# Expert panels of 1,792 features, a new block order and ring fill, and an fp32 first tile in the last gate

## The reference, cut to what matters

```python
def moe_swiglu(x, w_router, w_gate, w_up, w_down):
    logits = (x @ w_router).astype(jnp.float32)
    top_vals, top_idx = lax.top_k(logits, TOP_K)              # 2 of 8 experts
    weights = jax.nn.softmax(top_vals, axis=-1)
    ...
    for e in range(N_EXPERTS):
        out = out + combine[..., e:e + 1] * swiglu(x, w_gate[e], w_up[e], w_down[e])

# behind it, for layer i:
h = layer_norm(ALPHA * h + f, ln_g[i, 1], ln_b[i, 1])
h = h + jax.nn.sigmoid(h @ ple_w_gate[i] + ple_b_gate[i]) * (p[i] @ ple_w_proj[i])
```

## Time and profile before

| | us |
|---|---|
| three runs | 1474.23, 1474.25, 1471.96; median 1474.23 |
| the profiled execution | 1470.26 |
| its span, first to last instruction | 1468.5 |
| TensorE busy in the span | 1412.5 (96%) |
| VectorE busy | 702.5 (48%) |
| ScalarE busy | 319.8 (22%) |
| bytes moved by DMA | 467.99 MB, mean 319 GB/s |

### The profile page before, as it was taken

The page is one execution under the profiler, slowest core; times in us unless marked ns, Lnnn a source line. Parts: engine busy times, 40 slices in busy tenths (PEclk is TensorE's granted clock), DMA queues, the critical chain, the costliest instruction groups (busy, mean ns, idle before and its releaser), DMA issues.

```text
span 1468.5 us, 27721 instructions
## 1 busy us (share of the span) xinstructions
PE 1412.5 (96%) x12131; PEld 925.5 (63%) x12131; DVE 702.5 (48%) x1128; ACT 319.8 (22%) x432; POOL 24.6 (2%) x51
## 2 busy tenths in 40 slices
PE   8999999999999999999999999999999999999687
PEld 7888788888778877356666664456454454465135
DVE  4795678878874668432332332241422322323247
ACT  4444344344455553000000000000000000000012
POOL 3010000000000000000000000000000000000100
PEclk9999999999999999999999999999999999999998
DMA  9956445555456126999999999999999999999980
GB/s 367 337 197 248 165 172 183 189 200 185 166 177 207 50 78 262 419 412 404 416 414 419 420 419 420 419 418 421 419 419 420 419 420 419 420 420 415 417 348 30
DMA packets 135481, 467.99 MB, mean 319 GB/s; under 512 B 8524, under 2 KB 9376, under 8 KB 134848
## 3 DMA queue, kind: packets, MB, share of 16 engines
q1 hardware_dynamic: 130864, 450.92, 77.9%
q0 software_dynamic: 2992, 12.70, 2.3%
q10 hardware_dynamic: 1504, 2.62, 0.5%
HBM read 462.53 MB, written 3.67 MB: 317 GB/s over the span
## 4 chain that ended last, share of the span: by engine, by line
PE 78%; DMA 13%; DVE 5%; ACT 2%; issue 1%; SPq 1%; POOL 0%; ACTq 0%; POOLq 0%; DVEq 0%
PE ps L1781 76%; DMA ring<-in_moe_w_up_dram 10%; DMA ring<-in_moe_w_down_dram 2%; DMA raw<-in_ple_w_gate_dram 1%; DVE split L1121 1%; PE ps L1799 1%; ACT split L751 1%; DVE h L1169 1%; DVE stats L1173 1%; DVE acc L1164 1%; DVE htl L1136 0%; SPq L578 0%; PE ps L2116 0%; PE ps L2152 0%; DVE acc L1216 0%
## 5 line engine op out<-in xcount | busy, mean ns | idle before, releaser
L1781 PE MATMUL ps<-ring,xt 128*32 128x448 f32 x5632 | 546.2, 542 | 25.9 <-DMA ring<-in_moe_w_up_dram 25.6
L1781 PEld LDWEIGHTS ps<-ring,xt 128*32 128x32 f32 x5632 | 256.7, 110 | 300.0 <-issue 242.1
L1781 PE MATMUL ps<-split,hth 128*128 128x512 f32 x1168 | 366.7, 395 | 6.0 <-DVE htl L1136 2.8
L1699 DVE TENSOR_TENSOR m_hb<-ps,m_sg 128x224 f32<-128x224 f32 x88 | 29.2, 385 | 575.8 <-ACT m_sg L1054 575.8
L1781 PE MATMUL ps<-ring,m_bt 128*32 128x256 f32 (+1 forms) x3472 | 278.4, 469 | 6.8 <-DMA ring<-in_moe_w_down_dram 6.7
L1781 PEld LDWEIGHTS ps<-split,hth 128*128 128x128 f32 x1168 | 218.9, 190 | 53.8 <-DVE htl L1136 3.4
L1781 PEld LDWEIGHTS ps<-ring,m_bt 128*32 128x32 f32 x3472 | 173.0, 110 | 108.7 <-issue 28.8
L1781 PE MATMUL ps<-split,htl 128*128 128x512 f32 x584 | 229.3, 393 | 0.0
L1707 DVE STREAM_TRANSPOSE m_bt<-m_hb 32x224 f32<-32x224 f32 x352 | 205.1, 583 | 5.5
L1054 ACT ACTIVATE m_sg<-ps 128x224 f32<-128x224 f32 x88 | 25.4, 357 | 727.7 <-PE ps L1781 727.7
L1121 DVE TENSOR_TENSOR split<-raw,split 128x2048 fp32r<-128x2048 f32 x52 | 118.7, 2291 | 64.0 <-ACT split L751 63.9
(11 more groups left out here) (256 smaller groups left out, 651.1 us busy)
## 6 DMA issues: line engine op xcount, KB each, us to landing
ring<-in_moe_w_gate_dram SPq DMA_DIRECT2D x128, 896.0 KB, 17.2
ring<-in_moe_w_up_dram SPq DMA_DIRECT2D x128, 896.0 KB, 16.6
ring<-in_moe_w_down_dram SPq DMA_DIRECT2D x128, 896.0 KB, 16.2
raw<-in_gm_w_in_dram SPq DMA_DIRECT2D x14, 1024.0 KB, 14.6
raw<-in_ffn_w_gate_dram SPq DMA_DIRECT2D x14, 1024.0 KB, 5.0
raw<-in_ffn_w_up_dram SPq DMA_DIRECT2D x14, 1024.0 KB, 5.0
raw<-in_ffn_w_down_dram SPq DMA_DIRECT2D x14, 1024.0 KB, 5.0
raw<-in_fox_w_in_dram SPq DMA_DIRECT2D x12, 1024.0 KB, 4.9
```

The lines of the kernel that those rows point to most:

```text
L1699: ins = nc.vector.tensor_tensor(m_hb[:, q, :], ps[bank][:, QTR:2 * QTR], m_sg[:, q, :], ALU.mult)
L1781: return nc.tensor.matmul(o, a, b, start=start, stop=stop)
```

## The change

- **Panels.** `PANEL` goes from 896 to 1,792. There are 16 blocks instead of 32. A ring slot is one row of 1,792 floats for each of 128 partitions: before, a gate or up load filled a slot with two rows of 896 (256 input features); now it fills it with one row of 1,792 (128 input features). The bytes of a load and the loads of the down rows stay as they were. All gate slots of a block now stand ahead of its up slots, so gate and up have PSUM banks of their own (`gate_banks`, `up_banks`; a wide block's third up group reuses bank 0 after the silu of it). `m_hb` is gone: DVE writes the product back into `m_sg`. `m_bt` is single (only the last block has one of its own), so `turn_hidden(b)` waits for `down(b-1)`, and the silu of block `b` waits for `turn_hidden(b-1)`.
- **Order and gathering.** The first block of expert 6 is second, its other block seventh. The half of `xt` that holds experts 0, 6, 1 and 2 is gathered ahead of block 0; the other half behind `gate_up(1)`. `acc = ALPHA * h` is made behind that.
- **Fill.** `xh` lies over `acc` and `xl` over `par_b`; ring slots 13 to 15 wait for the router's logits (`lg_full`) instead of the gather; the first 16 loads are issued in the order `FILL`. `xh` and `xl` are made ahead of or within the routing.
- **The last gate.** Token tile 0 is copied unrounded (`ht`) and multiplied by `raw` in plain fp32; tile 1 stays a split product with four pairs `split1`. The tiles' norms stand directly behind each other on DVE, and a Sqrt ahead of `y_last` loads ACT's table early.

```diff
-PANEL = 896
+PANEL = 1792
-    SLOT = 2 * PANEL
-    X_BLK = 12
+    SLOT = PANEL
+    X_BLK = 24
...
+        order = [(e, j) for e in range(BIG) for j in range(NPAN)]
+        order.insert(1, (BIG, 0))
+        order.insert(6, (BIG, 1))
+        return order + [(NE - 1, j) for j in range(NPAN)]
...
-    xh, nxt = at("xh", [P, T, D], F32R, hth_at)
-    xl, _ = at("xl", [P, T, D], F32R, nxt)
+    xl, _ = at("xl", [P, T, D], F32R, par_b_at)
+    xh, _ = at("xh", [P, T, D], F32R, ph)
...
+    FILL = (0, 1, 2, 3, 4, 5, 10, 11, 12, 6, 7, 8, 9, 13, 14, 15)
...
             if end > SPLIT_END[-1]:
-                sp.wait_ge(gx_full, 2 * KD)
+                sp.wait_ge(lg_full, T)
...
+        act.wait_ge(s0["h"], H_NORM3 + 2)
+        nc.scalar.copy(xh[:, 0, :], h[:, 0, :]).then_inc(xh_ready, 1)
         tile_hi(1)
+        act.wait_ge(s0["h"], H_NORM3 + 2 * T)
+        nc.scalar.copy(xh[:, 1, :], h[:, 1, :]).then_inc(xh_ready, 1)
         small_out(3, 4, NE, slice(P, S))
...
             def turn_hidden(b):
+
                 dve.wait_ge(e_hid, hid0 + (b + 1))
+                if 0 < b < NB - 1:
+                    dve.wait_ge(s0["used"], used0 + (G_MOE + down_at(b - 1) + 8))
...
+                for which, banks in enumerate((gate_banks(b), up_banks(b))):
+                    for k in range(KD):
+                        slot = landed(gu_at(b) + which * KD + k)
                         for q, bank in enumerate(banks):
+                            if which == 1 and k == 0 and bank in gate_banks(b):
+                                pe.wait_ge(e_silu, silu0 + (3 * b + gate_banks(b).index(bank) + 1))
...
+                    gate_up(b)
+                    if b == HALF_1:
+                        pe.wait_ge(route_ready, 1)
+                        gather(1, at_e, gx0)
                         pe.wait_ge(gx_act, gx0 + KD)
                         pe.wait_ge(gx_dve, gx0 + KD)
...
+        def last_ple():
+
+            st = streams[1]
+            for nb in range(2):
+                bank = ps[GATE_BANKS[nb]]
+                for k in range(KD):
...
+                    last = mm(bank[:, :], ht[:, k, 0:P], raw[:, 2 * nb + k // 4, k % 4, :], k == 0, k == KD - 1)
+                last.then_inc(last_gate, 1)
+                if nb == 0:
+                    last_turn(1)
```

More of the change, by code:

```diff
@@ L891, in projected, with ple @@
                     .then_inc(proj_copied, 1)
-        def ple(which, g0, ready, last):
-            st = streams[which]
+        def ple(g0, ready, last):
+            st = streams[0]
             for nb in range(2):
@@ L1055, in experts @@
                         .then_inc(e_silu, 4 - len(banks) if q == len(banks) - 1 else 1)
+                if b == HALF_1:
+                    gathered(1, gx0)
+                if b == HALF_1 and r is None:
+                    act.wait_ge(gx_full, 2 * KD)
+                    for m in range(T):
+                        nc.scalar.mul(acc[:, m, :], h[:, m, :], ALPHA).then_inc(acc_init, 1)
                 if b and ORDER[b - 1][1] == NPAN - 1:
@@ L1204, in norm @@
                     scale_bias(h, acc, m, part, par[:, 2 * n + 1, part]).then_inc(streams[which]["h"], 1)
-            for q in range(2):
-                stream_lo(q, T - 1, which)
+            if which == 0:
+                for q in range(2):
+                    stream_lo(q, T - 1, which)
         def residual(k, g_end):
@@ L1413, in ple @@
                     if n < last:
[L1414 to L1426 removed]
+                        rest_lo(n)
@@ new lines, in ple @@
+                part = slice(nb * W, (nb + 1) * W)
+                dve.wait_ge(st["used"], g0 + 2 + 2 * nb)
+                for m in range(T):
+                    nc.vector.tensor_tensor(sig[:, m, part], ps[2 * (1 - nb) + m][:, :], ple_b[:, 0, part], ALU.add)\
+                        .then_inc(st["gb"], 1)
+                for m in range(T):
+                    dve.wait_ge(st["gs"], nb * T + m + 1)
+                    seq(nc.vector.tensor_tensor(sig[:, m, part], sig[:, m, part], pp[:, m, part], ALU.mult))
@@ L1608, in _ @@
         by_place(slots[:, :, 0:NE], slots_e)
-        def first_experts(half):
-            return slice(4 * half, 4 * half + 4)
-        select_every(first_experts, (0,))
-        rest_x(0)
-        select_every(first_experts, (1,))
+        for half in range(2):
+            select_half(half, lambda e, n: slice(e, e + n))
         def route_weights():
@@ L1741, in _ @@
             with dve.Fori(1, ROUNDS) as r:
-                rest_x(dve.snap(r * T))
-                select_every(lambda half: bass.ds(dve.snap(r * NE + 4 * half), 4))
-                gathered(r)
+                for m in range(T):
+                    rest_x(dve.snap(r * T), m)
+                for half in range(2):
+                    select_half(half, lambda e, n: bass.ds(dve.snap(r * NE + e), n))
+                gathered(0, dve.snap(r * (2 * KD)))
                 experts(r)
@@ new lines, in last_turn @@
+        def last_turn(m, between=None):
+            for q in range(2):
+                if q and between is not None:
+                    between()
+                pe.wait_ge(streams[1]["h"], 2 * m + q + 1)
+                if m:
+                    pe.wait_ge(streams[1]["tp_hi"], q + 1)
+                for c in range(4):
+                    last = nc.tensor.transpose(ps[6 + q][:, c * P:(c + 1) * P],
+                                               h[:, m, (4 * q + c) * P:(4 * q + c + 1) * P], ident[:, :])
+                last.then_inc(streams[1]["tp"], 1)
@@ L2308, in experts @@
                                              for n in (16 * CYC, NB, 2 * NE, 1, KD)]
+            silu0, at_e = [n if r is None else pe.snap(r * step + n) for step, n in ((3 * NB, 0), (2, 1))]
             def landed(n):
@@ L2343, in down @@
                         got += 1
-                    row = ring[:, first:first + 4].rearrange("p s n -> p (s n)")[:, c * D:(c + 1) * D]
+                    row = ring[:, first:first + 8].rearrange("p s n -> p (s n)")[:, c * D:(c + 1) * D]
                     if narrow(b):
                         for t in range(4):
-                            last = mm(ps[5][t * G3:(t + 1) * G3, :], m_bt[:, b % 2, t % 2, c, :],
+                            last = mm(ps[5][t * G3:(t + 1) * G3, :], bt[:, t % 2, c, :],
                                       row[:, t // 2 * W:(t // 2 + 1) * W], j == 0 and c == 0,
```

478 lines of the change are left out of this document (226 added, 252 removed).

## The result

The changed kernel takes 1454.61 us (median of 1453.79, 1454.77 and 1454.61) against 1474.23 before: a ratio of 0.987, 95% interval 0.9848 to 0.9893. Its profiled execution took 1453.79 us with a span of 1452.1, so the span fell by 16.4 us where the prediction had summed 20.3. The two slips, 3.9 us in the span and 3.2 in that distance, nearly cancel each other.

What follows compares the result with a forecast made beforehand. The ring's transfers, nearly level with TensorE, were taken to bound the experts. Gains of 16.3 us there and 4.0 in the tail sum to 20.3: span 1448.2, execution 1450.0, median 1454 beside 1474.23; range 1446 to 1468.

Steps and rivals of the forecast that it cites:

- the two large terms: Experts' transfers at 424 GB/s instead of 417 (814 us instead of 828), and a tail shorter by 4.0 us.
- the bounds of 1 and 6: Limits in us on the tail's predicted gain of 4.0: clock falling twice, or not at all.
- Term 1: Behind the first fill: three loads fewer left gain 6.6 us, a later restart of transfers costs 3.3; net gain 3.3.
- The register reads: SP's seven reads behind `placed`, 4.4 us, no longer hidden, so data restart at 589.8, 3.3 us later than before.
- 0.5 us of room: At load 32: its slot is free at 622.3, and it must be issued by 622.8 to keep the engines fed.
- any slip of the early phase counts in full: Up to load 32: no charge for a full ring, but every delay ahead of it adds fully to the time.
- The 2 us of wait ahead of block 1: TensorE waits 2 us for `hidden(0)` ahead of block 1; counted in TensorE's total, nothing charged to the end.
- the fall of the clock: At the start of the last gate: TensorE drops to the 1.2 GHz level, costing 1.7 us once instead of twice.
- Term 2: Experts' transfers: with every row of 7,168 bytes the rate becomes 424 GB/s, 814 us instead of 828 at 417.
- the low bound: Shortest time expected for one transpose of a 448 strip, 0.76 us; 1.17 was taken, 1.57 the high bound.
- rival 3: Wide blocks: silu, hidden and transpose chain becomes the bound, slower, 1493 us; chance 0.07 including other waits of the block cycle.
- Term 3: The tail behind the experts: new last gate ends at 1459.9 instead of 1463.8 in the old clock, gain 4.0 us.

Runs made afterwards that it cites:

- i_pieces: Changed kernel with every ring load issued as two transfers of 896 columns over all 128 rows, pieces of 3,584 bytes: 1468.60 us, ratio 0.9976.
- j_inter: Changed kernel with every ring load issued as two transfers of 64 rows, each taking every second row, pieces of 7,168 bytes: 1455.29 us, ratio 0.9883.
- d_fill: Changed kernel with ring slots 13 to 15 again waiting for the first gather's products instead of the router's logits: 1453.22 us, ratio 0.9865.
- a_numbers: Changed kernel with DVE's three operations that find the experts' numbers moved ahead of the copies of the first gather: 1454.12 us, ratio 0.9873.
- b_busy: Changed kernel with longer TensorE fillers (54 and 54 dummy products, not 26 and 20) in the two waits ahead of the first gather: 1451.73 us, ratio 0.9863.
- e_third: Changed kernel with the narrow block third instead of second: 1463.11 us, ratio 0.9935.
- k_three: Changed kernel with longer fillers, early expert numbers, and other PSUM banks so block 1 need not wait for hidden(0) at its start: 1451.08 us, ratio 0.9855.
- c0_after: The changed kernel itself, unaltered, measured again: 1454.25 us, ratio 0.9878.
- g_halves: Changed kernel with every ring load issued as two transfers, rows 0 to 63 and rows 64 to 127: 1917.56 us, ratio 1.3.
- c_both: Changed kernel with both the longer TensorE fillers and the experts' numbers found ahead of the first gather's copies: 1452.40 us, ratio 0.9867.
- h_tail: Kernel before the change with the new last gate alone (old panels, order and fill): 1467.12 us, ratio 0.996.

## Why the prediction came out as it did

**The sign and the size were right, by the reasons given for the two large terms.** The rate rose to the 424 GB/s that was read off the windows of down rows, and i_pieces and j_inter show that the size of the pieces did it. The tail gave 5.9 us, within the bounds of 1 and 6. In the span, 3.9 us less came than was summed: the last down product came 5.8 us later than forecast, and the tail behind it was 1.9 us shorter. Two slips in the sums themselves changed nothing: 1463.8 less 1459.9 is 3.9 and not 4.0, and a rate of 428 with a tail of 6 gives about 1444.4 instead of 1446 for the lower end of the range.

**Term 1 failed as a whole, at the step "are set by when they restart behind the first fill, by how many bytes are left then".** Three loads fewer behind the gather were worth 6.6 us in the sum and nothing on the chip (d_fill). The register reads took 4.25 us (forecast 4.4), were charged with 3.3 and cost nothing (a_numbers). Part of that charge was wrong in itself: the first packets of the 17th load start at 590.13, 1.0 us behind its issue, where the sum had 2.4. Both terms failed for one cause: between the restart and load 32 the ring is nearly empty of orders, since every load waits for a slot of block 0, 2.26 us apart, while a load needs 2.16 us at 424 GB/s. Whatever is saved ahead of load 32 is waited for there. The prediction had seen the place ("0.5 us of room") and charged nothing; in truth it was short by 1.35 us, because TensorE came to it 1.8 us later than predicted. The step behind it, that any slip of the early phase counts in full, held: b_busy took the slip away and the end moved with it. e_third shows the rest of that paragraph right too: it is the narrow block that makes it up. The 2 us of wait ahead of block 1, which the paragraph counted and charged with nothing, were worth 1.2 us (k_three).

**`gate_up(0)` started at 584.41, not 582.6.** Of these 1.8 us, 0.8 were there ahead of the routing already. The chain of the kernel before has its 48 products there at

```profile
556.32 6.91 PE ps L1781 x48
```

and the changed kernel at 557.12. The distance is as large where the long piece of layer 0 begins (25.53 and 26.36, and 25.39 to 26.65 in the other kernels), so this is what executions differ by. From that mark on the routing and the gather took 27.3 us, against 27.7 before and 26.3 in the forecast. The 1.0 us too many have a cause that is larger than they are. TensorE waits for the routing twice (the rests are now made in it), the clock was granted at half from 573.2 to 580.0, and the first six pairs of the gather stand at 0.64 us instead of 0.35: 1.7 us. This term was missing; without it b_busy took 25.5, 0.8 less than forecast, so the other terms of the early phase were charged too high by that much, and the runs do not say which. The prediction looked for the fall of the clock in the tail, where it stayed away, and did not look for it here.

**The stretch was to be 821.3 us (582.6 to 1403.9) and is 825.3.** 1.35 us are the shortage at load 32. 2.1 are the two windows at 1400 to 1410. 0.6 remain, a balance: the transfers began sooner behind the 17th issue than was summed, and small dips took more than that (423 GB/s from 700 to 1020). With 1.8 from the start this makes the 5.8 us by which 1409.7 is later than 1403.9.

For the two windows at the end there is no experiment, but the trace says what they are. From 1400 on the engines are partly idle (share 0.89 and 0.86) although the last down load lands only at 1409.7; c0_after reads 376 and 293 GB/s there, k_three 277 at 1400 to 1405. A load counts its semaphore up in 16 steps, as many as there are engines, and the trace has the time of each. For the last down load six of the 16 stand at 1397.99 to 1399.21, two at 1401.97 and 1402.32, and eight only at 1407.72 to 1409.69. So some shares of a load are done up to 11.7 us ahead of the last. (That one step is one engine's share is a reading of the count.) The distance grows during the run, from 3.9 us in the median between 600 and 1020 to 7.6 between 1020 and 1300. Before it was 9.4 us for the last down load, with 349 GB/s in the last five microseconds ahead of 1420. What drives the shares apart is open.

**Term 2** needed no repair. The page counts 102,710 packets where the page of before has 135,481: 32,771 fewer, predicted 32,768. By the rule of the Trainium skill ("DMA: Bandwidth & Descriptors", "Why small descriptors are slow (HBM only)") the estimate was 422.6 GB/s; the trace reads 424, and between all small and all large pieces 414 and 423, 2.2% where the rule has 1.3%. The other rule that the prediction weighed, from the section "Where 436 GB/s comes from" of the same page of the Trainium skill, that the HBM side binds at about 358 GB/s, did not hold here: the long window of the changed kernel reads 424.

**TensorE and the transposes.** A transpose took 954 ns, between the low bound (0.76) and the value taken (1.17). From 653.23 to 1341.45 TensorE waits for nothing, so the single `m_sg` and `m_bt` cost nothing there and rival 3 did not occur. That the engines are at a share of 1.02 in the same time shows the two level with each other; here, too, a busy share alone would not have said which one sets the pace.

**Term 3** was 5.9 us for 4.0. The first fp32 product came 11.85 us behind the last down slot's (predicted about 12), at 0.44 us an instruction (0.43). 1.7 of the 1.9 us of difference had been set aside for a fall of the clock, which stayed at 1.00.

## What to carry to other kernels

A transfer that is issued when a buffer comes free is paced by whoever frees the buffer until the queue has run full once. So, before crediting a restart or a fill, find the load at which the two paces cross, and ask what comes later there; all that is saved ahead of it is lost again. And when bytes are the bound, look at the contiguous run per row first: doubling it gave about 8.5 of 16 us here by the estimate above. Of the waits that the larger panel and its order could have brought, one shows in the chain, 1.70 us ahead of block 1, worth 1.2.

## What the runs showed of the hardware that was not expected

**Rows 0 to 63 and 64 to 127 as two transfers run at little more than half the rate.** g_halves read 233 GB/s at 700 to 800 and 276 at 1020 to 1380 with all engines busy; the same bytes, the same number of transfers and rows, but every second row (j_inter) read 423. The Trainium skill has this in "SBUF — State Buffer", "Door 1: The DMA port swizzle": rows 0 to 63 reach eight of the sixteen ports, and by its section "Can I just issue two DMAs to hit both halves?" a second transfer to the other half does not help. The trace agrees at 700 to 800 (233 is 0.55 of 423) and less well later (276 is 0.65). That page says one transfer must span all 128 partitions for all ports; in j_inter two transfers of 64 of them each, spread over the range, did as well as one of 128 (423 GB/s beside 424).

**Waits of about 2 us ahead of the gather can halve TensorE's clock for 3 to 7 us.** In the changed kernel TensorE waits 2.00 us for DVE until 572.35 and 1.93 us until 576.13, with fillers of 1.71 us between; the granted clock was half (the 1.2 GHz level) from 573.2 to 580.0. All nine traces here with both waits (the first 2.0 us, the second 1.4 to 2.2) show it, 6.8 us long. With fillers that left 0.44 and 0.47 us of waiting (b_busy, c_both, k_three) it stayed at the 2.4 GHz level. A single wait is not safe either. The kernel before waited 2.09 us once, until 572.62, and kept the full clock, but h_tail, with the same work of TensorE and the same wait there, was at half from 574.1 to 577.5, and the first twelve instructions of its gather took 3.86 us instead of 2.32:

```profile
574.14 3.86 PE L1798 MATMUL ps<-every,xh 128*128 128x384 f32 x12 [2.09 <-DVE every L1570]
```

So a wait that costs nothing itself, since another engine is the one that works, can cost 1.5 to 1.9 us behind its end, and the same work of TensorE can go either way.
